# A decoder layer with top-2 of 32 experts on one core: experts' rows accumulated into the residual in DRAM, one-pass final norm, 4 KB weight pieces, output-weight scaling spread over a solver's levels

## The reference

```python
mod = silu(c) @ w_ada + b_ada                       # six vectors: shift, scale, gate, twice
h = rms_norm(x, g1) * (1 + sc1) + sh1
p = h @ w_in                                        # 4 groups: pooling, windowed attention, short conv, RWKV-7
x = x + gt1 * (concat(ya, yb, yc, yd) @ w_out)
h = rms_norm(x, g2) * (1 + sc2) + sh2
# router: best of 4 groups, best 2 of its 8 experts, gates = softmax(top 2) * group probability
act = silu(h @ w_gate[e]) * (h @ w_up[e]) * gate    # D -> 128 per expert
x = x + gt2 * sum_over_its_two_experts(act @ w_down[e])
out = rms_norm(x, final_g)
```

## Time and profile before

| | |
|---|---|
| median of 3 executions | 1004.54 us (996.2 to 1005.4) |
| the profiled execution | 996.17 us, span 994.4 us |
| busy share of PE, DVE, ACT, POOL | 87%, 50%, 25%, 30% |
| mean granted clock of TensorE | 0.924 of full |
| DMA traffic | 136.31 MB, mean 137 GB/s |
| chain that ended last | PE 71%, DVE 11%, DMA 6% |

### The profile page before, as it was taken

One profiled execution on the slowest core, in us unless ns is written; L12 is line 12 of the kernel. 1 busy time (PEld: TensorE's weight loads), 2 busy tenths in 40 slices (PEclk: granted clock), 3 DMA queues, 4 the chain that ended last, 5 costly groups with the idle time before them and its releaser, 6 DMA issues.

```text
span 994.4 us, 16926 instructions
## 1 busy us (share of the span) xinstructions
PE 864.1 (87%) x6842; PEld 581.7 (58%) x6842; DVE 499.4 (50%) x1169; ACT 246.7 (25%) x608; POOL 303.1 (30%) x409
## 2 busy tenths in 40 slices
PE   5999996999999977897979699999659999999800
PEld 5554453555544436886868445555458888788600
DVE  4820588677611035657564314444545555555447
ACT  5220221223101023443434111212122222222112
POOL 4800065000670002433422000000124565544235
PEclk9889997999999987898989799999769999999965
DMA  9823433453011031000000193100458999998566
GB/s 345 235 72 106 127 106 106 139 173 111 22 43 43 22 115 57 3 3 3 3 2 4 60 343 127 43 21 25 136 153 267 293 289 308 312 315 264 179 247 263
DMA packets 140004, 136.31 MB, mean 137 GB/s; under 512 B 18365, under 2 KB 119962, under 8 KB 139930
## 3 DMA queue, kind: packets, MB, share of 16 engines
q1 hardware_dynamic: 129770, 118.46, 37.4%
q0 software_dynamic: 10160, 16.81, 4.8%
HBM read 127.85 MB, written 25.75 MB: 154 GB/s over the span
## 4 chain that ended last, share of the span: by engine, by line
PE 71%; DVE 11%; DMA 6%; issue 5%; POOL 3%; ACT 2%; SPq 1%; POOLq 0%; DVEq 0%; ACTq 0%
PE bank L719 67%; DMA REG_Y<-xn_d,idx 3%; DVE REG_Y L1532 2%; PE bank L1204 2%; DMA REG_Y<-in_x 1%; POOL rs L516 1%; DVE REG_Y L1992 1%; PE bank L969 1%; ACT REG_W L1249 1%; POOL ss L515 1%; DMA REG_P<-in_moe_w_down 1%; PE bank L831 1%; PE bank L1151 1%; DMA y_d<-REG_Y,idx 1%; SPq L446 1%
## 5 line engine op out<-in xcount | busy, mean ns | idle before, releaser
L719 PE MATMUL bank<-REG_W 128*128 128x512 f32 (+1 forms) x864 | 284.8, 521 | 11.4 <-DVE pend L1760 6.9
L719 PEld LDWEIGHTS bank<-REG_W 128*128 128x128 f32 (+1 forms) x864 | 125.6, 183 | 156.6 <-issue 146.1
L719 PE MATMUL bank<-REG_W,REG_Y 128*128 128x512 f32 x276 | 129.0, 606 | 1.1 <-DVE REG_Y L1985 1.1
L1249 ACT ACTIVATE REG_P<-bank 128x256 f32<-128x256 f32 (+2 forms) x126 | 57.4, 462 | 192.0 <-PE bank L719 148.3
L719 PE MATMUL bank<-REG_P 64*64 64x64 f32 (+1 forms) x2816 | 92.1, 230 | 10.9 <-DVE REG_P L1802 6.9
L719 PEld LDWEIGHTS bank<-REG_P 64*64 64x64 f32 x2816 | 86.6, 141 | 17.3 <-DVE REG_P L1802 8.5
L719 PE MATMUL bank<-REG_Y,REG_W 128*128 128x128 f32 (+1 forms) x800 | 88.4, 277 | 2.1 <-DVE REG_Y L1871 2.1
L719 PEld LDWEIGHTS bank<-REG_Y,REG_W 128*128 128x128 f32 (+1 forms) x800 | 84.6, 184 | 8.4 <-issue 8.4
L719 PEld LDWEIGHTS bank<-REG_W,REG_Y 128*128 128x128 f32 x276 | 50.1, 194 | 48.5 <-issue 48.5
L1249 ACT ACTIVATE REG_Y<-bank,mod,s 128x128 f32<-128x128 f32 x132 | 49.8, 457 | 88.0 <-PE bank L1204 88.0
L1532 DVE SCALAR_TENSOR_TENSOR REG_Y<-REG_P,cc,REG_Y 128x256 f32<-128x256 f32 x112 | 64.1, 572 | 4.0
(11 more groups left out here) (283 smaller groups left out, 1112.0 us busy)
## 6 DMA issues: line engine op xcount, KB each, us to landing
REG_P<-in_w_ada SPq DMA_DIRECT2D x18, 1024.0 KB, 6.2
REG_W<-in_moe_w_gate SPq DMA_DIRECT2D x21, 512.0 KB
REG_W<-in_moe_w_up SPq DMA_DIRECT2D x21, 512.0 KB
REG_W<-in_moe_w_down SPq DMA_DIRECT2D x21, 512.0 KB
REG_W<-in_w_in SPq DMA_DIRECT2D x17, 512.0 KB
REG_W<-y_d SPq DMA_DIRECT2D x14, 512.0 KB
REG_P<-in_w_ada SPq DMA_DIRECT2D x3, 2048.0 KB, 12.2
REG_P<-in_moe_w_gate SPq DMA_DIRECT2D x12, 512.0 KB
```

The costliest lines, as they stand in the source:

```text
L719: return pe.matmul(o_, l, r, start=start, stop=stop, skip_group_check=True)
L1249: return act.activation(o_, i_, f, **kw)
```

## The change

- `y_d` now has T rows and starts as `x1`: SP stores each residual tile to it in stage 4. A scatter adds `yo` to the token's row (`compute_op=ALU.add`). Since a token has two experts, each scatter waits until the one before has landed. The tables lose the column for the place in the old `y_d`, indices are read from `tbl` itself, and copy and `junk` before each indirect DMA go (not in the overflow loop).
- The last stage loads one tile of `y_d` into `x1`, squares, takes the roots for two tiles at a time and scales in place.
- Gate and up weights are loaded with 8 consecutive rows of D to a partition, 4 KB pieces. D is thus permuted in everything that meets them: transposes of `x1` and the columns for shift 2 and scale 2 read SBUF with a step of 8 floats, ACT writes the normed rows permuted.
- The 16 scalings of the output weights move between the levels, one behind each of `bl` 1 to 4 in every turn.
- v is centred as it is turned, by a matmul with `cen` = I - bones/64, and `mean_sums` and `centred` go. The three small products become one step, `loras`, at level 3, their matmuls interleaved over banks 5, 6, 7; ACT's `out_gate` comes ahead of `rates`.

```diff
-        wg_v = v["moe_w_gate"].rearrange("l e (k p) f -> p (l e) k f", p=P)
+        wg_v = v["moe_w_gate"].rearrange("l e (p k) f -> p (l e) (k f)", k=KD)
...
                 sp.dma_start(xn2_d[j * P:(j + 1) * P, :], xn2[:, j % 2]).then_inc(s_st[j % 2], 16)
+                sp.dma_start(y_d[j * P:(j + 1) * P, :], x1[:, j]).then_inc(s["st_x1"], 16)
...
-                for n in range(2):
-                    sp.dma_start(yab[j][:, n], y_d[n * T + j * P:n * T + (j + 1) * P, :]).then_inc(s_w[j], 16)
+                sp.dma_start(x1[:, j], y_d[j * P:(j + 1) * P, :]).then_inc(s_w[j], 16)
...
+                    if m == 0 and l == 1:
+                        gp.wait_ge(s["wo_ld"], 32)
+                        gp.wait_ge(s["mod2_ready"], 8)
+                    if l < 5:
+                        k, h = 2 * m + (l - 1) // 2, (l - 1) % 2
+                        gp.tensor_tensor(wo_at(k, h), wo_at(k, h), gtb[:, 0, h * 512:(h + 1) * 512], ALU.mult).then_inc(s["wo_sc"], 1)
                 if m + 1 < TURNS:
                     norm_power(front_norm(m + 1))
-                if m == 0:
-                    gp.wait_ge(s["wo_ld"], 32)
-                    gp.wait_ge(s["mod2_ready"], 8)
-                for k in ((0, 1, 2), (3, 4, 5), (6, 7), ())[m]:
-                    for h in range(2):
-                        gp.tensor_tensor(wo_at(k, h), wo_at(k, h), gtb[:, 0, h * 512:(h + 1) * 512], ALU.mult).then_inc(s["wo_sc"], 1)
...
+            def scatter_add(at, par, done):
+
+                gp.indirect_dma_start(out=y_d[:, :], out_offset=bass.IndirectOffsetOnAxis(ap=at, axis=0),
+                                      in_=yo[:, par], in_offset=None, bounds_check=last_row,
+                                      oob_is_err=False, compute_op=ALU.add).then_inc(done, 16)
...
+                gp.wait_ge(s["m_yd"], e + 1)
+                if e >= 1:
+                    gp.wait_ge(s_sc[(e - 1) % 2], 16 * ((e - 1) // 2 + 1))
+                scatter_add(rows_of(e, 0), e % 2, s_sc[e % 2])
...
-                    last = columns(PS[6][:, 0:4], acb.rearrange("p a b -> p (a b)"), 4)
+                    strided = acb.rearrange("p a (q k) -> p k (a q)", k=KD)
+                    for k in range(KD):
+                        last = mm(PS[6][64 * half:64 * half + 64, k:k + 1], strided[:, k, :], ones[:, 0:1])
...
+            def loras(m):
+
+                pe.wait_ge(s["w_tanh"], m + 1)
+                pe.wait_ge(s["w_sg"], m + 1)
                 if m > 0:
                     pe.wait_ge(s["w_w1"], m)
+                    pe.wait_ge(s["w_bon"], m)
+                    pe.wait_ge(s["w_nbu"], front_norm(m - 1))
                 for p in range(2):
+                    at, wide = slice(p * W2, (p + 1) * W2), slice(p * P, (p + 1) * P)
+                    mm(PS[5][:, at], lor[64:128, wide], lt[64:128, :])
+                    mm(PS[6][:, at], lor[0:32, wide], lt[0:32, :])
+                    last = mm(PS[7][:, at], lor[32:64, wide], pT[32:64, B_LORA, PAD + m * W2:PAD + (m + 1) * W2])
                 last.then_inc(s["w_lora"], 1)
...
-                flip_in(2, lambda p, tk: pT[:, B_V + p, PAD + m * W2 + tk.start:PAD + m * W2 + tk.stop], 0)
+                for n in range(2):
+                    for p in range(2):
+                        t0 = PAD + m * W2 + n * P
+                        last = mm(PS[2][:, (2 * n + p) * P:(2 * n + p + 1) * P], pT[:, B_V + p, t0:t0 + P], cen[:, :])
+                last.then_inc(s["w_tok"], 1)
...
+                strided = x1[:, j].rearrange("p (q k) -> p k q", k=KD)
                 for k in range(KD):
-                    last = pe.transpose(PS[4 + k // 4][:, (k % 4) * P:(k % 4 + 1) * P], x1[:, j, k * P:(k + 1) * P],
-                                        ident[:, :])
+                    last = pe.transpose(PS[4 + k // 4][:, (k % 4) * P:(k % 4 + 1) * P], strided[:, k, :], ident[:, :])
...
-                stt(yab[j][:, 0], x1[:, j], rs[:, 2, j:j + 1], fg, ALU.mult, ALU.mult).then_inc(s["f_o"], 1)
+            def root_args(i):
+                dve.wait_ge(s["ss_ready"], 2 * NT + 2 * i + 2)
+                at = slice(2 * i, 2 * i + 2)
+                ts(ss[:, 2, at], ss[:, 2, at], EPS, None, ALU.add).then_inc(s["f_ss"], 1)
+
+            root_args(0)
+            for i in range(NT // 2):
+                if i + 1 < NT // 2:
+                    root_args(i + 1)
+                dve.wait_ge(s["rstd_ready"], 2 * NT + i + 1)
+                for j in (2 * i, 2 * i + 1):
+                    stt(x1[:, j], x1[:, j], rs[:, 2, j:j + 1], fg, ALU.mult, ALU.mult).then_inc(s["f_o"], 1)
```

More of the change, by code:

```diff
@@ L650, in gather @@
                 pause()
+                return idx[:, col:col + 1]
+            def gather(tile, par, done):
+                at = rows_of(tile, 0)
                 gp.indirect_dma_start(out=xg[:, par], out_offset=None, in_=xn2_d[:, :],
-                                      in_offset=bass.IndirectOffsetOnAxis(ap=idx[:, par:par + 1], axis=0),
-                                      bounds_check=last_row, oob_is_err=False).then_inc(s_gx[par], 16)
-            def scatter(e, par):
-                row_ = e if isinstance(e, int) else gp.snap(e)
-                gp.wait_ge(s["m_yd"], e + 1)
-                ch.step(gp.tensor_copy(idx[:, 2 + par:3 + par], tview(row_, 0)))
-                pause()
-                gp.indirect_dma_start(out=y_d[:, :], out_offset=bass.IndirectOffsetOnAxis(ap=idx[:, 2 + par:3 + par], axis=0),
-                                      in_=yo[:, par], in_offset=None, bounds_check=last_out,
-                                      oob_is_err=False).then_inc(s_sc[par], 16)
@@ L664, in gather_overflow @@
[L664 to L670 removed]
+                                      in_offset=bass.IndirectOffsetOnAxis(ap=at, axis=0),
@@ L847, in outputs, with sums @@
                 last.then_inc(s["att_o"], 1)
-            def sums(nb, gates):
+            def sums(nb, gates, half=0):
                 pe.wait_ge(s["acb_ready"], nb * 2 + 2)
@@ L1033, in turn @@
                         blocks(n, n, bl[:, l % 2], lambda i, r: xx[r, i, :], "w_t1p")
-                    if more and l == 2:
-                        lora_w(m + 1)
                     if tail and l == 3:
@@ L1038, in turn @@
                     if more and l == 3:
-                        lora_a(m + 1)
+                        loras(m + 1)
                     if tail and l == 4:
-                        norm_back(tail_norm(m - 1), m)
+                        if more:
+                            wait("w_gg", 1, 2)
+                        norm_back(tail_norm(m - 1))
                     if more and l == 4:
                         norm_sums(front_norm(m + 1), sq)
-                        lora_g(m + 1)
                     for n in range(2):
@@ L1425, in turn @@
                     if more and l == 3:
+                        out_gate(m + 1)
                         rates(m + 1)
-                    if more and l == 4:
-                        out_gate(m + 1)
                 for n in range(2):
```

217 lines of the change are left out of this document (83 added, 134 removed).

## The result

The changed kernel takes 1056.23 us (median of 4 executions, 1055.92 to 1058.75) against 1000.51 us for the kernel before (median of 4 executions, 996.2 to 1005.4); the ratio is 1.056, 95% interval 1.049 to 1.063. It is slower, where 973 us was forecast. Its profiled execution took 1056.12 us, span 1053.0, so 58.6 us more than the 994.4 of before.

What follows compares the result with a forecast made beforehand. PE was taken as the bound (71% of the chain). RWKV -10.1, projection +2, routing -1.2, expert loop -2 and overflow with last stage -15.2 sum to -26.5 us: 969.7 from 996.17, stated as 973 us, range 958 to 992.

Steps and rivals of the forecast that it cites:

- the first rival: Expert loop: each scatter waits for the previous landing; at 8.0 us +57 us, 1030 us; chance slower 0.07, between 0.13.
- The point that decides: Expert loop: scatter waits cost once issue to landing L exceeds 6.17 us, one expert's time; loss 31 x (L - 6.17).
- Last stage: After the experts: half the loads and two of three DVE passes go, 19.8 us instead of 35.7, -15.9 us.
- Overflow: Overflow tile's scatter must land before the last loads start; with its data moved twice, +0.7 us.
- The scalings: RWKV turns 1 and 2: spreading them shortens DVE's path to PE's restart from 5.65 to 2.57 us; -6.2 us together.
- The sign I named for it: RWKV turns 1 and 2: PE's wait at level 5 would fall below 0.7 us, from 3.26.
- The rest of RWKV: Apart from scalings: mean_sums -3.1 us, earlier squares -1.9, centring matmuls +1.2, small products -1.1; turn 0's start +1.0.
- The small products: RWKV levels: one piece costs 2.26 us, ends 1.13 and 3.4, net -1.1; ahead of turn 0 +1.0, ends 0 and 2.07.
- Projection: Shift 2 and scale 2 columns: 16 passes instead of 8 at four places, +2 us, ends 0 and +3.9.
- that rival: Strided weight loads of x1_turned in routing: doubled and not hidden, they cost +9 us, 982 us; chance 0.13.
- Routing: Last tile and first gather: fewer small DVE operations, no index copy and junk, -1.2 us together; residual stores 0.
- 4 KB pieces: Expert loop: cheaper weight loads and earlier gathers close PE's holes, -2 us, ends -3.7 and 0.

Runs made afterwards that it cites:

- slots: Changed kernel with plain, unchained scatters into two rows per token, residual kept in SBUF and the old last stage: 1002.59 us, ratio 1.004.
- spread_only: Kernel before with only the output-weight scalings spread, one behind each of levels 1 to 4 of turns 0 to 3: 991.88 us, ratio 0.9933.
- plain_chain: Changed kernel with scatters plain instead of accumulating, still chained: 1000.37 us, ratio 1.004.
- light_loads: Changed kernel with expert-weight loads from expert 8 on carrying only 16 of 128 partitions, scatters still accumulating and chained: 1010.88 us, ratio 1.011.
- two_targets: Changed kernel with odd experts accumulating into a second, zeroed buffer, each scatter waiting for the one two before, last stage adding both: 1022.71 us, ratio 1.025.
- plain_light: Changed kernel with plain, chained scatters and expert-weight loads from expert 8 on of only 16 of 128 partitions: 981.25 us, one execution.
- spread_cen: Kernel before with the scalings spread and v centred by a matmul, mean_sums and its DVE pass gone: 992.95 us, ratio 0.994.
- cols_contig: Changed kernel with the shift 2 and scale 2 column passes reading 64 neighbouring weights, giving wrong column order: 1075.69 us, one execution, with a second overflow tile.
- last_acc: spread_cen with half the results added onto the residual in SBUF by eight accumulating gathers in the last stage, scatters plain and unchained: 1002.64 us.

## Why the prediction was wrong

**The step that failed** is in the first rival, where the accumulating scatter is priced: "The nearest row is the plain scatter of the same rows; with its data moved twice and the traffic of the loop I put it at 5.5 us, and the wait costs nothing." Scatters land in 7.7 us at the median instead of 5.5, and POOL waits for each of the 31 behind the first, 154.6 us in all. The mechanism and its place were on record, with a chance of 0.07; the size put into it was wrong. The nearest row was taken by the transfer's form (the plain scatter, 3.2 us on an idle machine) and not by the traffic around it. The gather among the weight loads, 8.0 us, was at hand as the upper end. Even where no weights are loaded, 5.5 us is too little: the last two scatters of the changed kernel take 5.94 and 5.90 us from issue to landing. In slots, a plain scatter in the loop lands in 7.6 us at the median. In the kernel before nobody waited for it, so it cost nothing and no row showed it; the change was what made it cost.

**The point that decides** was set too high as well, and the formula 31 x (L - 6.17) lacks a term. The step is the landing plus 0.7 us until POOL has issued the next scatter, so the wait begins to cost at 5.5 us, not at 6.17. The value taken stood on that edge, without a margin. With the median landing of 7.7 the formula gives +47 us; with the measured step in place of L it gives 31 x (8.49 - 6.17) = +72 us of the stage's +75.8. Another 2.4 us lie between the first gather and the first scatter (25.95 against 23.6 us).

**Last stage**: right, -18.3 against -15.9; the last store ends 4.2 us behind the last scaling instead of 5.8, which makes 1.6 of the difference. **Overflow**: last scatter of the loop to the first load is 13.76 us, 13.79 before, so the +0.7 did not show as a sum. The addition did cost more, 4.7 us to landing instead of 2.6, but the overflow's scatter came 8.04 us behind the loop's last instead of 9.81: the loop's last scatter had itself been late. That the two cancel is luck.

**The scalings**: right. From DVE's first `tensor_scalar` to PE's restart it is 2.58 us in turn 1 (462.31 - 459.73), where the earlier trace rows give 5.65 and the prediction 2.57. The sign I named for it, a wait below 0.7 us, was wrong: it is 2.78 us, since the third small product (1.13 us) no longer stands in front of it and DVE's path behind the norm's sums is long by itself. In spread_only, where that product is still in its place, the wait is 1.73 us. How long PE waits depends on how much of its own work lies beside the path, so the path's length is the better sign.

**The rest of RWKV** came only in part: -4.5 us against -11.1. The mean's matmul went (1.02 us a turn) and the `cen` matmuls came (1.16 us against 0.66), but some starts of turns ran at the lower clock for longer. The start of turn 3, before and after:

```profile
518.00:526.00 8.00, 7.94 (x150) 6.33 (x150) 6.02 (x9) 3.44 (x7) 3.46 (x2) 1.00 0.01 2
```

```profile
522.40:530.40 8.00, 7.93 (x98) 6.74 (x100) 5.05 (x7) 2.28 (x4) 4.54 (x3) 0.71 0.01 2
```

PE is busy for all of both; the granted clock is 1.00 (2.4 GHz) in one and 0.71 on average in the other, which passes from 1.2 to 2.4 GHz within it. The products there take 1.98 instead of 1.10 us. From turn 3's start to its last level it is 25.62 us instead of 23.86, where the terms had -0.7. The execution decides over this clock, at least within the changed code: plain_chain and light_loads have the same RWKV code, take 1.10 us for turn 3's first products like the kernel before, and need 179.7 and 180.2 us from turn 0 to the router (-6.8 and -6.4), while in slots, two_targets and plain_light these products take 1.98 to 1.99 us and the stretch 182.4 to 185.6. In each of these profiles a gain stays, in none is it the 11.1 forecast. Whether the change makes the low clock likelier is open: spread_only's profile shows it at the same starts, and its runs are still 6.7 us faster; spread_cen's runs give the centring nothing.

**The small products** cost 2.51 us in the levels (448.88 to 451.39), near the 2.26 taken: wide and narrow ones do not overlap. The ends had been 1.13 and 3.4. Ahead of turn 0 they took 3.40 us (372.08 to 375.48), and the norm's sums came 2.1 us later, at the end named (2.07).

**Projection**: +6.0 us against +2 with 3.9 as the upper end. Of it 1.7 us are not the passes: from the third place to the fourth it is 21.73 us at a mean granted clock of 0.92, from the second to the third 20.03 at 1.00; the kernel before has 18.72 at 1.00 for both. All six profiles with strided columns have this stretch of lower clock, and neither the kernel before nor cols_contig has it; what brings it about is not shown. The bound from eight passes assumed that only the number of passes changes; cols_contig shows that the step of the reads costs more than their number. I had weighed the step at `x1_turned` and not here. There a load rose from 0.141 to 0.192 us

```profile
L1134 PEld LDWEIGHTS bank<-ident,REG_P x64: 185/192/206, 593.2 to 712.5; 128*128 128x128 f32 x64
```

and hides under 0.27 us of matmul: tiles are 17.3 us apart in both kernels, so that rival is refuted, at the place it named. The columns move a single float, nothing covers their weight loads, and at full clock the same step shows whole. The Trainium skill, Advanced Engine Details and Errata, SBUF Cachelines, states a penalty for reads that meet a new 16-byte line each time; the trace agrees (2.08 against 1.09 us), but only where the load is not covered.

**Routing**: -3.5 against -1.2, and most of the difference is luck. At the last tile it is 3.49 us from DVE's last `x1` to PE's next products (710.36 to 713.85), where it was 5.37 (705.97 to 711.34): -1.9. The operations that fill `hots` give the -0.3 that I had counted. The other 1.6 us are two operations on `lanes`, before and after:

```profile
709.22 2.07 DVE L1927 TENSOR_SCALAR lanes<-i,place 128x128 f32<-128x128 f32 x2
709.34 1.80 POOL L629 MEMSET REG_Y<- 128x2048 f32 x1
```

```profile
713.31 0.48 DVE L1900 TENSOR_SCALAR lanes<-i,place 128x128 f32<-128x128 f32 x2
713.74 1.80 POOL L633 MEMSET REG_Y<- 128x2048 f32 x1
```

Beside POOL's filling of `REG_Y` they take 2.07 us; 0.3 us earlier they are through before it starts. It is the crowding of the earlier trace rows at another place, where I had not looked for it; slots, whose `hots` has its third column back, has the 2.07 again. From there to the table's products it is -1.2, to the first gather -0.3, where copy and `junk` had been put at 0.9: copy and `junk` began 0.32 us behind the table's last operation, and the gather itself now begins 1.05 us behind it. **4 KB pieces**: the -2 us for the loop's holes does not come even in slots, where the scatters are as before: between 780 and 900 us PE is busy for 116.80 us there and for 118.60 in the kernel before.

## What to carry to other kernels

A transfer that nobody waits for can have a long landing time that costs nothing and stands in no row, as the scatters did here; before making anyone wait for it, price it from transfers that run in the same traffic, and add the time from landing to the next issue. Accumulating in DRAM turned independent writes into a chain here and took DMA time as well, so it wants a loop with both to spare: it saved 18 us at the end and cost 76 on the way. A strided operand cost nothing under matmuls of 128 columns and doubled passes of one column at full clock, so ask at each place what covers it.

## What the runs showed of the hardware

- A scatter of 128 rows of 4 KB lands in 3.2 us behind the last weight loads, an accumulating one in 5.9 to 6.0 there and in 6.2 at the median beside light traffic (light_loads); beside whole weight loads a plain one takes 6.1 (plain_chain) to 7.6 (slots), an accumulating one 7.7. POOL's own instruction is 1.59 us instead of 1.00.
- With two accumulating scatters allowed in flight the DMA engines move 285 GB/s at a busy share of 0.92, with plain ones 327 at 0.91 (two_targets, slots).
- Accumulating gathers of 512 KB from DRAM into SBUF, four in flight, land one each 3.8 us (last_acc).
- Weights read with a step of 32 bytes: 16 loads of 64 columns take 2.00 us instead of 1.01, and 2.00 as well at half the granted clock; loads of 128 columns 0.192 us instead of 0.141.
- Two DVE operations of 128x128 take 2.07 us beside a `MEMSET` of 128x2048 on POOL and 0.48 us without it.
